# Router logits and expert rows from scaled rows, with the norm applied as a column per token

## The chip, the cores and the metric

The kernel runs on one core of one Trainium2 chip. The metric is the device time of one execution in microseconds. The kernel before was run three times: 1560.26 us is the median (1556.66 to 1560.38).

## What is computed

One inference step of a small diffusion backbone: two layers, 128 context tokens and 256 latent tokens, model width 1024. All is float32. Each layer has an attention branch and a recurrent branch, merged and projected with `w_out`, and then a mixture of experts. What matters here is the step into the experts:

```python
x = x + g1 * (merged @ lp['w_out'])
h2 = _rmsnorm(x, lp['norm2']) * (1 + sc2) + sh2
x = x + g2 * _moe(h2, router_w, router_b, lp['w_gate_up'], lp['w_down'])
```

`_rmsnorm` divides each token's row by its root mean square (rms) and multiplies by a gain per column. `sc2` and `sh2` are vectors per stream (context and latent) that come from a modulation product. In `_moe`, sigmoid scores of `h2 @ router_w` pick one group of four experts and in it two of 16 experts for each token. The expert is SwiGLU with 512 hidden columns. The modulation vectors of a layer come from twelve chunks of a product with `w_ada`; the gains and shifts of the first norm of a layer are chunks 0 to 3.

## The kernel before, in words

The kernel is written by hand, engine by engine. Each engine has a program in order, and semaphores (`wait_ge`, `then_inc`) link them. Line numbers are those of the profile.

- Activations are kept transposed: `xT` and `hT` are [128 partitions, 8 column tiles, 384 tokens]. Large products are done in three parts with a high and a low half of each operand. ScalarE rounds the weights to the high half (L1071, L1269), VectorE subtracts to get the low half (L1547, L1901).
- `w_ada`, `w_in` and the projections come as chunks of 2 MB into three slots of `ring`. Expert weights come as pieces of 1 MB into eight spots; six of these are halves of the ring slots, two lie in `parts`. SP issues all of these loads in the order of `chunk_order`, each when the last user of its spot is done (L481 to L484).
- Product results go through three banks `G`, taken in the order of `gemm_order`; transposes and small sums go through two banks `TB`, in the order of `tran_order`. The reader of a bank increments `gbank_read` or `tbank_read`, and TensorE waits for that before it uses the bank again.
- The output stage of a layer is three rows of eight split products (L545): `ap` (attention), `rp` (recurrent) and `wo` (output). `ADA_AFTER` puts modulation products (L555) and their sums (L564) between them.
- After each `wo` product VectorE adds it to `xT` (L1738) and squares the tile (L1742); TensorE sums the squares over partitions with a matrix of ones (L571), one product behind.
- After `wo` 7 the chain is: the last sum of squares, the root on ScalarE (`rms`, L1046), the load of the Exp table (L1231), the reciprocal of the [128, 384] tile `rs` (L1511), eight multiplications into `hT` (L1518), gain and shift on GpSimd for the context tokens (L2028) and on ScalarE for the latent ones (L1081), eight router products with 32 columns of weights (L777), a copy (L1237), the turn back to token rows (L791) and the sigmoid's exponential (L1249). Then VectorE routes: some fifty small steps from L1755 to L1855.
- Meanwhile TensorE does modulation products 2 and 3 of the next layer and their sums (layer 0), or five filler products (layer 1, `run_on`, L520: products whose result nobody reads).
- TensorE also transposes `hT` to token rows (24 transposes in six groups, L785); ScalarE copies each group (L1245) and stores the rows to `h2_rows` in DRAM (L1253, three stores).
- The rank of each token in its expert (L806) and the token of each place (L814) come from small products; L819 places the gates. Then GpSimd gathers the 128 rows of each expert with an indirect DMA (L2047). Unused places gather row 0. TensorE transposes them (L827), ScalarE copies (L1274), and the first expert product starts (L855, L861).
- The results of 14 experts are stored to `expert_rows`, those of the last two are kept on chip. At the end GpSimd gathers for each token the two rows (six indirect DMAs, L2060; picks of the kept experts read row 0 with gate 0), ScalarE and VectorE combine them (L1309, L1956), and TensorE transposes them (L959) and adds the kept experts (L964).

Of the kernel before, what the change touches and what calls it, by code (L numbers as in the profile page):

```python
# [33 lines left out]
CAP = 128  # L34
HELD = 2
# [90 lines left out]
def gemm_order():  # L126

    o = [(0, "ada", c) for c in ADA_START]
    for l in range(DEPTH):
# [28 lines left out]
def tran_order():  # L158
# [3 lines left out]
    for l in range(DEPTH):  # L162
# [6 lines left out]
        if l + 1 < DEPTH:  # L169
            o += [(l + 1, "mod", c) for c in ADA_FIRST]  # L170
# [10 lines left out]
def build(nc, x_prompt, x_sample, cache_k, cache_v, state_h, c, c_ctx, norm1_g, norm2_g, w_ada, b_ada,  # L181
# [4 lines left out]
    with ctx:  # L186
# [80 lines left out]
        shift_k = sb("shift_k", [P, KVH, 2])  # L267
        slot_gate = sb("slot_gate", [P, EVEN])
# [66 lines left out]
        same_b = tmp[:, 0, 0:6 * EVEN].rearrange("p (i b) -> p i b", i=6)  # L335
        hot_f = hot_c.bitcast(F32)
        gate_b = tmp[:, 1, 0:6 * EVEN].rearrange("p (i b) -> p i b", i=6)
# [8 lines left out]
        h2d = nc.dram_tensor("h2_rows", (T, D), F32, kind="Internal").ap()  # L346
        yd = nc.dram_tensor("expert_rows", (SENT * CAP, D), F32, kind="Internal").ap()

# [155 lines left out]
        def _(pe):  # L504
# [119 lines left out]
            for l in range(DEPTH):  # L624
# [6 lines left out]
                def h_ready(k):  # L631
                    pe.wait_ge(S("h_ready_p"), 2 * l * KT + k + 1)
                    pe.wait_ge(S("h_ready_a"), 2 * l * KT + k + 1)
# [114 lines left out]

                pe.wait_ge(S("att_split"), (l + 1) * HEADS)
                for name, high, low in (("ap", parts_r[:, 0], parts_r[:, 1]), ("rp", qT_r, gr_r),  # L750
                                        ("wo", parts_r[:, 0], parts_r[:, 1])):
                    for n in range(KT):
# [5 lines left out]
                        if n and name == "wo":  # L758
                            square_sum(gr, n - 1, slice(0, T), sq_base + n)
                        for plan, do in ((ADA_SUM_AFTER, mod_sum), (ADA_AFTER, modulation)):  # L760
# [11 lines left out]
                bank = g_take((l, "logits", 0))  # L772
                for k in range(KT):
                    pe.wait_ge(S("h_ready_p"), (2 * l + 1) * KT + k + 1)
# [1367 lines left out]
```

## Time and profile before

| | |
|---|---|
| median of 3 runs | 1560.26 us (1556.66 to 1560.38) |
| profiled execution | 1560.94 us |
| its span, first to last instruction | 1559.1 us |
| TensorE busy | 1496.3 us, 96% |
| VectorE busy | 1116.7 us, 72% |
| ScalarE busy | 921.6 us, 59% |
| GpSimd busy | 161.2 us, 10% |
| mean granted TensorE clock | 0.986 |
| moved by DMA | 373.00 MB, 239 GB/s on average |

The busy share is an average over stages. A stage's limit is read from the chain of waits: followed back from the last instruction, it gives at each moment the work that the end depended on. The granted clock is in parts of full speed (2.4 GHz).

### The profile page before, as it was taken

What the parts mean: (1) busy time and instruction counts of PE and PEld (TensorE: products, weight loads), DVE (VectorE), ACT (ScalarE), POOL (GpSimd) and SP (SyncE); (2) the same over time, 40 slices, a digit from 0 to 9 for tenths busy, and PEclk for the clock granted to TensorE, in tenths of its full rate; (3) what the DMA queues carried; (4) which work ended last, traced back from release to release, by engine and by line L of the source; (5) the groups of instructions that cost most, each with busy time, mean ns of one, the idle gap of its engine ahead of it and who ended that gap; (6) DMA issues with size and microseconds to landing.
All of it is one profiled execution on the core that took longest, in us unless ns stands there. A gap on an engine that the chain in (4) does not pass through costs nothing.

```text
span 1559.1 us, 19489 instructions
## 1 busy us (share of the span) xinstructions
PE 1496.3 (96%) x7375; PEld 1196.6 (77%) x7375; DVE 1116.7 (72%) x1717; ACT 921.6 (59%) x1176; POOL 161.2 (10%) x218
## 2 busy tenths in 40 slices
PE   6999999999998999999999999999999899999996
PEld 4699866679875788888769987666989478888885
DVE  4447656774646999999874665777464689999986
ACT  1233569972224877787742355999321577878774
POOL 0100012200011000000240000221000201000002
PEclk9999999999999999999999999999999999999999
DMA  9455433214667999999755553113240799999983
GB/s 348 172 201 199 147 108 112 68 56 162 216 224 293 360 401 410 409 407 406 290 189 194 191 186 140 63 63 113 97 174 12 288 355 408 413 412 406 406 346 122
DMA packets 132708, 373.00 MB, mean 239 GB/s; under 512 B 9217, under 2 KB 12673, under 8 KB 132609
## 3 DMA queue, kind: packets, MB, share of 16 engines
q1 hardware_dynamic: 113728, 326.57, 55.7%
q0 software_dynamic: 10432, 25.18, 4.6%
q10 hardware_dynamic: 8448, 19.94, 3.2%
q8 instruction: 62, 1.02, 0.3%
q14 instruction: 38, 0.30, 0.1%
HBM read 351.71 MB, written 19.94 MB: 238 GB/s over the span
## 4 chain that ended last, share of the span: by engine, by line
PE 78%; DVE 7%; ACT 5%; DMA 5%; issue 4%; POOL 1%; SPq 0%; POOLq 0%; DVEq 0%; ACTq 0%
PE bank L545 24%; PE bank L855 19%; PE bank L861 10%; PE bank L534 10%; PE bank L555 2%; DMA ring<-in_w_ada 2%; PE bank L743 2%; PE bank L827 2%; PE bank L716 1%; PE bank L571 1%; DMA expert_rows<-gb 1%; PE bank L653 1%; PE bank L648 1%; PE bank L564 1%; DMA tmp<-expert_rows,posu 1%
## 5 line engine op out<-in xcount | busy, mean ns | idle before, releaser
L1901 DVE TENSOR_TENSOR spot_low<-spot,piece_high 128x2048 fp32r<-128x2048 f32 x192 | 433.4, 2286 | 31.5 <-ACT piece_high L1269 30.5
L1269 ACT ACTIVATE piece_high<-spot 128x2048 fp32r<-128x2048 f32 x192 | 366.5, 1917 | 42.4 <-PE bank L861 40.3
L855 PE MATMUL bank<-piece_high,ga_r 128*128 128x512 f32 x768 | 308.8, 402 | 3.0 <-ACT ga_r L1286 1.4
L855 PE MATMUL bank<-spot_low,ga_r 128*128 128x512 f32 x768 | 301.6, 393 | 0.0
L861 PE MATMUL bank<-piece_high,ga_r 128*128 128x512 f32 x768 | 210.7, 396 | 0.0
L545 PE MATMUL bank<-parts_r,ga_r 128*128 128x384 f32 x768 | 202.6, 345 | 0.0
L534 PE MATMUL bank<-hT,ring 128*128 128x384 f32 x544 | 185.0, 494 | 4.4 <-ACT ga L1212 2.3
L855 PEld LDWEIGHTS bank<-piece_high,ga_r 128*128 128x128 f32 x768 | 144.3, 188 | 37.9 <-ACT ga_r L1274 2.2
L861 PEld LDWEIGHTS bank<-piece_high,ga_r 128*128 128x128 f32 x768 | 144.2, 188 | 34.5
L855 PEld LDWEIGHTS bank<-spot_low,ga_r 128*128 128x128 f32 x768 | 144.6, 188 | 30.6
L534 PEld LDWEIGHTS bank<-hT,ring 128*128 128x128 f32 x544 | 102.1, 193 | 71.2 <-issue 4.1
L545 PEld LDWEIGHTS bank<-parts_r,ga_r 128*128 128x128 f32 x768 | 138.3, 188 | 5.9 <-issue 5.0
L545 PE MATMUL bank<-parts_r,gb_r 128*128 128x384 f32 x384 | 129.7, 338 | 0.0
L545 PE MATMUL bank<-parts_r,hT_r 128*128 128x384 f32 x384 | 100.4, 342 | 0.0
L2047 POOL DMA_INDIRECT gr<-h_rows,ids x32 | 45.3, 1417 | 457.4 <-PE bank L827 423.7
L545 PE MATMUL bank<-parts_r,ring_r 128*128 128x384 f32 x256 | 87.9, 343 | 0.0
L1547 DVE TENSOR_TENSOR gb_r<-ring,ga_r 128x1024 fp32r<-128x1024 f32 x48 | 58.5, 1222 | 35.3 <-ACT ga_r L1071 33.7
L2040 POOL DMA_DIRECT2D gatew<-in_lru_wa x64 | 34.0, 536 | 465.3 <-PE bank L743 465.1
L545 PEld LDWEIGHTS bank<-parts_r,gb_r 128*128 128x128 f32 x384 | 72.1, 188 | 0.0
L545 PEld LDWEIGHTS bank<-parts_r,hT_r 128*128 128x128 f32 x384 | 69.4, 188 | 2.5
L1042 ACT ACTIVATE tmp<-bank 128x512 f32<-128x512 f32 x24 | 14.4, 598 | 83.7 <-PE bank L555 83.7
L1071 ACT ACTIVATE hT_r<-ring 128x1024 fp32r<-128x1024 f32 x36 | 37.1, 1052 | 36.6 <-PE bank L545 36.6
(314 smaller groups left out, 2351.7 us busy)
## 6 DMA issues: line engine op xcount, KB each, us to landing
spot<-in_w_gate_up SPq DMA_DIRECT2D x128, 1024.0 KB, 8.1
spot<-in_w_down SPq DMA_DIRECT2D x64, 1024.0 KB, 8.2
ring<-in_w_ada SPq DMA_DIRECT2D x24, 2048.0 KB, 8.1
ring<-in_w_in SPq DMA_DIRECT2D x22, 2048.0 KB, 8.1
expert_rows<-gb ACTq DMA_DIRECT2D x28, 512.0 KB, 6.9
ring<-in_w_attn_proj SPq DMA_DIRECT2D x4, 2048.0 KB, 8.3
ring<-in_w_rnn_proj SPq DMA_DIRECT2D x4, 2048.0 KB, 10.0
ring<-in_w_out SPq DMA_DIRECT2D x4, 2048.0 KB, 12.5
```

The costliest lines, as they stand in the source:

```text
L534: mm = pe.matmul(bank[:, 0:width], slot_kn(slot)[:, k, n * P:(n + 1) * P], rhs(k), start=(k == 0), stop=(k == KT - 1))
L545: mm = pe.matmul(bank[:, 0:T], w[:, k, :], x[:, k, :], start=(k == 0 and i == 0), stop=(k == KT - 1 and i == 2))
L555: mm = pe.matmul(bank[g:g + 32, :], cpad[:, k, :], slot_kn(s)[:, k, :], start=(k < 4), stop=(k >= 4), tile_position=(0, g))
L743: pe.matmul(bank[:, 0:CW], gatew[:, which, n % 2, :], xc[:, j, :], start=True, stop=True).then_inc(S("gemm_done"), 1)
L855: pe.matmul(out[n], high[:, 2 * q + k, :], w[:, k, n * 512:(n + 1) * 512], start=(q == 0 and k == 0 and i == 0), stop=False)
L861: mm = pe.matmul(out[n], low[:, 2 * q + k, :], w_high[:, k, n * 512:(n + 1) * 512], start=False, stop=(q == pieces - 1 and k == 1))
L1071: ac.activation(w_high_part(kind, n), slot_kn(s)[:, :, n % 4 * P:(n % 4 + 1) * P], ACT.Copy)\
L1269: ac.activation(highs[p % HIGHS], spots[u], ACT.Copy).then_inc(S("piece_high"), 1)
L1547: ve.tensor_tensor(low, slot_kn(s)[:, :, n % 4 * P:(n % 4 + 1) * P], high.bitcast(F32), ALU.subtract)\
L1901: ve.tensor_tensor(spots_low[u], spots[u], highs[p % HIGHS].bitcast(F32), ALU.subtract)\
L2040: po.dma_start(gatew[half * 64:half * 64 + 64, which, n % 2, half * 64:half * 64 + 64], w[l, d, 2 * j + half]).then_inc(S(f"gatew_loaded{n ...
L2047: po.indirect_dma_start(out=dst, out_offset=None, in_=h2d[:, :], in_offset=bass.IndirectOffsetOnAxis(ap=idx, axis=0)).then_inc(sem, 16)
```

## The change

- The norm is no longer applied to `h2` before the router. After each `wo` product, GpSimd (context) and ScalarE (latent) write the tile times gain into `xc` (`scaled`). The eight router products read `xc` and follow `wo` 7; the last sum of squares stands between the seventh and the eighth.
- The rms row is turned into a column per token with three one-row products; VectorE takes the reciprocal of [128, 3] (`rstd_c`). The exponential takes it as its scale, and `sel_e` has a minus sign. ScalarE's copies of the transposed rows take it as their scale.
- The shift enters as one-row products of the rms row with a row of shift values: for the logits `bias_row`, for the token rows `shift_row`. They are prepared in the `rp` stage: the router's product with the shift after `rp` 0 (`shift_logits`), its sum after `rp` 3 (`bias_turned`), and two transposes of the shift, copied by VectorE, stored to DRAM by ScalarE at `rp` 6 and loaded back as one row at `wo` 4.
- The six groups of transposes accumulate a product of one row and 512 columns each.
- Modulation products 2 and 3 of the next layer move from ahead of the router to behind the rank product (in place of four filler products in layer 0), their sums to behind the gate product, in place of one filler product. In layer 1 the five fillers ahead of the router go, and two of the last ones stay of three. The two fillers before the rank go in both layers. ScalarE's copies of the two products stand behind the first high piece of expert 0; VectorE's additions stand behind `slot_gate`.
- The gathers get a bounds check: unused places have an index past the last row (`NOWHERE`) and are not fetched; in the last gathers the picks of the kept experts are not fetched.

```diff
@@ gemm_order, tran_order
+        o.append((l, "logits", 0))
         if l + 1 < DEPTH:
             o += [(l + 1, "ada", c) for c in (2, 3)]
-        o.append((l, "logits", 0))
...
         o += [(l, "ids", 0)]
+        if l + 1 < DEPTH:
+            o += [(l + 1, "mod", c) for c in ADA_FIRST[2:4]]
@@ TensorE
+                def shift_logits():
+                    pe.wait_ge(S("exp_done"), (l + 1) * len(UNITS))
+                    t_read(pe, (l, "mod", 7))
+                    for k in range(KT):
+                        g = 32 * (k % 4)
+                        mm = pe.matmul(SB[0][g:g + 32, 0:2], rw[:, k, :], modT[:, 24 + k, :],
+                                       start=(k < 4), stop=(k >= 4), tile_position=(0, g))
+                    for st in range(2):
+                        mm = pe.transpose(SB[0][0:KT, (st + 1) * P:(st + 2) * P], modT[:, 24:32, st], ident)
+                    mm.then_inc(S("shift_logits"), 1)
+
+                def bias_turned():
+                    pe.wait_ge(S("bias_part"), l + 1)
+                    for st in range(2):
+                        mm = pe.matmul(SB[0][0:1, 16 + st * NE:16 + (st + 1) * NE], bias_part[:, st:st + 1], sel_e,
+                                       start=True, stop=True, skip_group_check=True)
+                    mm.then_inc(S("bias_turned"), 1)
...
+                for k in range(KT - 1):
+                    raw_logits(k)
                 square_sum(gr, KT - 1, slice(0, T), sq_base + KT).then_inc(S("ss_done"), 1)
-                if l + 1 < DEPTH:
-                    modulation(l + 1, 2)
-                    modulation(l + 1, 3)
-                    mod_sum(l + 1, 2)
-                    mod_sum(l + 1, 3)
-                else:
-                    run_on(SB[1], 5)
...
+                raw_logits(KT - 1).then_inc(S("gemm_done"), 1)
+
+                pe.wait_ge(S("rms_ready"), 2 * l + 2)
+                for t in range(TT):
+                    mm = pe.matmul(SB[1][:, t:t + 1], rs[0:1, t * P:(t + 1) * P], ones[0:1, 0:1],
+                                   start=True, stop=True, skip_group_check=True)
+                mm.then_inc(S("rms_turned"), 1)
+                g_read(pe, (l, "logits", 0))
+                pe.wait_ge(S("bias_known"), l + 1)
+                for t in range(TT):
+                    st = 0 if t == 0 else 1
+                    out = SB[0][:, t * NE:(t + 1) * NE]
+                    pe.matmul(out, lpart[:, t * P:(t + 1) * P], sel_e, start=True, stop=False, skip_group_check=True)
+                    mm = pe.matmul(out, rs[0:1, t * P:(t + 1) * P], bias_row[:, st * NE:(st + 1) * NE],
+                                   start=False, stop=True, skip_group_check=True)
+                mm.then_inc(S("logits_turned"), 1)
+
+                pe.wait_ge(S("shift_back"), 16 * (l + 1))
+                for i in range(2 * TT):
+                    t, half = divmod(i, 2)
                     bank = t_take((l, "h2", i))
                     for k in range(4):
+                        pe.matmul(bank[:, k * P:(k + 1) * P], xc[:, half * 4 + k, t * P:(t + 1) * P], ident,
+                                  is_transpose=True, start=(k == 0), stop=False, skip_group_check=True)
+                    pe.matmul(bank[:, :], rs[0:1, t * P:(t + 1) * P], shift_row[:, min(t, 1), half * 512:(half + 1) * 512],
+                              start=False, stop=True, skip_group_check=True).then_inc(S("tran_done"), 1)
...
-                run_on(SB[1], 2, T)
...
-                run_on(SB[1], 4)
+                if l + 1 < DEPTH:
+                    modulation(l + 1, 2)
+                    modulation(l + 1, 3)
+                else:
+                    run_on(SB[1], 4)
...
-                run_on(SB[1], 3)
+                if l + 1 < DEPTH:
+                    mod_sum(l + 1, 2)
+                    mod_sum(l + 1, 3)
+                run_on(SB[1], 2)
                 xturn(0)
@@ ScalarE
+                def scaled(k):
+                    g_read(ac, (l, "wo", k))
+                    ac.activation(xc[:, k, CTX:T], xT[:, k, CTX:T], ACT.Copy, scale=modA[:, 1, k, 1:2])\
+                        .then_inc(S("router_a"), 1)
...
+                ac.wait_ge(S("rstd_known"), l + 1)
+                ac.wait_ge(S("logits_turned"), l + 1)
+                for t in range(TT):
+                    ins = ac.activation(rt[:, 0, t, :], SB[0][:, t * NE:(t + 1) * NE], ACT.Exp, scale=rstd_c[:, t:t + 1])
+                ins.then_inc(S("logits_exp"), 1)
...
-                for q in range(3):
-                    piece_high("gu0", q)
+                piece_high("gu0", 0)
+                if l + 1 < DEPTH:
+                    ada_copy(l + 1, 2)
+                    ada_copy(l + 1, 3)
+                piece_high("gu0", 1)
+                piece_high("gu0", 2)
@@ VectorE
-                normed()
-                if l + 1 < DEPTH:
-                    mod_add(l + 1, 2)
-                    mod_add(l + 1, 3)
-                    ve.nop().then_inc(S("first_mods"), 2)
-
+                bank = g_ready(ve, (l, "logits", 0))
+                ve.tensor_copy(lpart, bank[:, 0:T]).then_inc(g_free((l, "logits", 0)), 1)
+                ve.wait_ge(S("rms_turned"), l + 1)
+                ve.reciprocal(rstd_c[:, :], SB[1][:, 0:TT]).then_inc(S("rstd_known"), 1)
@@ GpSimd
-                modulated(1)
+                for k in range(KT):
+                    g_read(po, (l, "wo", k))
+                    po.tensor_scalar(xc[:, k, 0:CTX], xT[:, k, 0:CTX], modA[:, 1, k, 0:1], None, ALU.mult)\
+                        .then_inc(S("router_p"), 1)
...
                     po.indirect_dma_start(out=dst, out_offset=None, in_=h2d[:, :],
-                                          in_offset=bass.IndirectOffsetOnAxis(ap=idx, axis=0)).then_inc(sem, 16)
+                                          in_offset=bass.IndirectOffsetOnAxis(ap=idx, axis=0),
+                                          bounds_check=T - 1, oob_is_err=False).then_inc(sem, 16)
```

## Rows read from the trace of the kernel before

**Rows 1.** Busy time by windows, in the experts: PE, PEld, DVE, ACT, POOL, PEclk, DMA, GB/s

```profile
600.00:700.00 100.00, 100.00 (x468) 81.67 (x467) 91.85 (x56) 78.82 (x56) 7.29 (x6) 1.00 1.02 408
```

**Rows 2.** Chain of waits, layer 0: start us, us, what

```profile
455.04 0.75 DVE xT L1738 x2
...
456.43 0.93 PE bank L571 x2
...
457.90 2.56 DVE hyb L1511
...
464.16 4.07 PE bank L777 x14
...
468.86 0.86 PE bank L791 x6
...
469.98 0.20 DVE pt L1755
...
477.24 0.25 DVE pt L1814
...
482.05 0.81 PE bank L814 x6
...
488.57 0.89 PE bank L827 x8
...
490.56 2.13 PE bank L855 x8
```

**Rows 3.** Chain of waits, layer 1

```profile
1205.43 0.75 DVE xT L1738 x2
...
1220.01 0.20 DVE pt L1755
...
1232.10 1.23 PE bank L814 x6
...
1240.25 0.89 PE bank L827 x8
...
1242.23 2.12 PE bank L855 x8
```

**Rows 4.** Timeline, layer 0, ScalarE and VectorE: start, us, engine, line, operation

```profile
457.89 1.28 ACT L1231 ACT_TABLE_LOAD   x1
...
484.34 4.48 DVE L1901 TENSOR_TENSOR spot_low<-spot,piece_high 128x2048 fp32r<-128x2048 f32 x2
```

**Rows 5.** Timeline, layer 0, TensorE

```profile
469.55 1.07 PE L785 MATMUL bank<-con,hT 128*128 128x128 f32 x8
...
476.44 3.68 PE L520 MATMUL bank<-con 128*128 128x512 f32 x8
```

**Rows 6.** Gathers (layer 0), last store (layer 1), its landing, gathers' landing

```profile
483.71 1.05 POOL L2047 DMA_INDIRECT gr<-h_rows,ids  x1 [16.66 <-DVE ids L1857]
...
485.06 2.41 POOL L2047 DMA_INDIRECT gr<-h_rows,ids  x1 [0.30 <-issue]
...
1224.04 0.33 ACTq L1253 DMA_DIRECT2D h_rows<-gr  x1
...
h_rows<-gr ACTq DMA_DIRECT2D x1, 512.0 KB, 8.2
...
DMA to landing us min/median/max: 4.1/7.7/10.3
```

**Rows 7.** Chain of waits, rnn projection stage, layer 1

```profile
1151.35 12.76 PE bank L545 x72
```

**Rows 8.** Timeline, layer 0, end of the experts: GpSimd and TensorE

```profile
777.72 0.94 POOL L2060 DMA_INDIRECT tmp<-expert_rows,posu  x1 [0.30 <-issue]
...
786.23 0.30 PE L959 MATMUL bank<-con,gb 128*128 128x128 f32 x1 [1.33 <-DVE tmp L1956]
```

**Rows 9.** Busy time by windows, columns as in rows 1

```profile
465.00:467.00 2.00, 2.00 (x10) 0.79 (x10) 0.66 (x5) 0.50 (x2) 2.00 (x5) 0.50 1.03 414
1232.00:1234.00 2.00, 1.90 (x10) 1.93 (x11) 0.43 (x3) 0.00 (x0) 0.17 (x1) 0.58 0.03 8
```

More of the change, by code:

```diff
@@ L34 @@
 CAP = 128
+NOWHERE = 512
 HELD = 2
@@ L169, in tran_order @@
         if l + 1 < DEPTH:
-            o += [(l + 1, "mod", c) for c in ADA_FIRST]
+            o += [(l + 1, "mod", c) for c in ADA_FIRST[0:2]]
         o += [(l, "h2", i) for i in range(2 * TT)]
@@ L779, in _, with raw_logits @@
-                mm.then_inc(S("gemm_done"), 1)
-                def h2_rows(i):
+                logits = g_take((l, "logits", 0))
+                def raw_logits(k):
+                    pe.wait_ge(S("router_p"), l * KT + k + 1)
+                    pe.wait_ge(S("router_a"), l * KT + k + 1)
+                    g = 32 * (k % 4)
+                    return pe.matmul(logits[g:g + 32, 0:T], rw[:, k, :], xc[:, k, 0:T],
+                                     start=(k < 4), stop=(k >= 4), tile_position=(0, g))
@@ L790, in _ @@
-                for t in range(TT):
-                    mm = pe.matmul(OB[:, t * NE:(t + 1) * NE], lpart[:, t * P:(t + 1) * P], sel_e,
-                                   start=True, stop=True, skip_group_check=True)
-                mm.then_inc(S("logits_turned"), 1)
-                for i in range(1, 2 * TT):
-                    h2_rows(i)
+                        pe.matmul(bank[:, k * P:(k + 1) * P], xc[:, half * 4 + k, t * P:(t + 1) * P], ident,
+                                  is_transpose=True, start=(k == 0), stop=False, skip_group_check=True)
@@ L869, in xturn @@
                         for b in range(2):
-                            pe.wait_ge(S(f"tbank_read{b}"), len(range(b, T_AT[(l, "ids", 0)] + 1, 2)))
+                            last = T_AT[(l + 1, "mod", 3) if l + 1 < DEPTH else (l, "ids", 0)]
+                            pe.wait_ge(S(f"tbank_read{b}"), len(range(b, last + 1, 2)))
                     else:
@@ L878, in gu @@
                     if e == 0:
-                        done = G_AT[(l, "logits", 0)]
+                        done = G_AT[(l + 1, "ada", 3) if l + 1 < DEPTH else (l, "logits", 0)]
                         for b in range(2):
@@ L1503, in mod_add @@
                     link(ve.tensor_copy(modA[:, 3, kk:kk + 4, :], m))
-            norms = [0]
-            def rstd():
-                norms[0] += 1
-                ve.wait_ge(S("rms_ready"), norms[0])
-                link(ve.reciprocal(rs, rs))
             for l in range(DEPTH):
-                def normed():
-                    rstd()
-                    for k in range(KT):
-                        ve.tensor_tensor(hT[:, k, :], xT[:, k, :], rs, ALU.mult).then_inc(S("xn_ready"), 1)
                 if l == 0:
@@ L2020, in _ @@
             for l in range(DEPTH):
-                def modulated(which):
-                    base = (2 * l + which) * KT
-                    for k in range(KT):
-                        if which == 0 and k % 4 == 0:
-                            po.wait_ge(S("first_mods"), 2 * l + k // 4 + 1)
-                        po.wait_ge(S("xn_ready"), base + k + 1)
-                        po.tensor_scalar(hT[:, k, 0:CTX], hT[:, k, 0:CTX], modA[:, which, k, 0:1],
-                                         modT[:, which * 24 + k, 0:1], ALU.mult, ALU.add).then_inc(S("h_ready_p"), 1)
-                modulated(0)
+                for k in range(KT):
+                    if k % 4 == 0:
+                        po.wait_ge(S("first_mods"), 2 * l + k // 4 + 1)
+                    po.wait_ge(S("xn_ready"), l * KT + k + 1)
+                    po.tensor_scalar(hT[:, k, 0:CTX], hT[:, k, 0:CTX], modA[:, 0, k, 0:1],
+                                     modT[:, k, 0:1], ALU.mult, ALU.add).then_inc(S("h_ready_p"), 1)
                 for n, (d, j) in enumerate(PAIRS):
```

105 lines of the change are left out of this document (57 added, 48 removed).

## The prediction

> **What bounds the kernel now.** I read the busy time by windows first: in the middle of the experts TensorE is busy for all of 100 us [rows 1]. The DMA engines are full there too, but a piece of weights is requested only when TensorE has given a spot back, so TensorE sets the pace, and fewer gathered bytes give nothing in that stretch. The change has to pay elsewhere: in the stretch between the last output product of a layer and its first expert product. There I read the chain of waits [rows 2, 3]. In both layers it is serial: one engine works, the next waits. From the update of x after product wo 7 (call its start T0: 455.04 and 1205.43) to the first expert product there are 490.56 - 455.04 = 35.5 us in layer 0 and 1242.23 - 1205.43 = 36.8 us in layer 1. The routing on VectorE starts at T0 + 14.94 and T0 + 14.58.
>
> **Removed: the norm ahead of the router.** Before, the chain from T0 is: update and square 1.39, last sum of squares and root 1.47, reciprocal of the 128x384 tile 2.56, normalising, modulating and the eight router products until 468.16, a copy, the turn back 0.86, the exponential, VectorE at 469.98 [rows 2]. The new chain, from the same rows:
> - Seven of the eight raw router products run while VectorE updates and squares tile 7. They are 14 instructions. Six products of the turn back took 0.86 with their drain, some 0.12 apart. So they need 1.6 us and have a gap of 1.39; the sum of squares starts at T0 + 1.55. The bounds of the delay are 0 and 0.6: GpSimd may scale tile 7 first and hold up the squaring, and its steps paced seven router products in 4.07, 0.58 each [rows 2].
> - Sum and root, 1.47: T0 + 3.0.
> - rms turned into columns: three one-row products, six instructions like the turn back, 0.8 to the last. The logits need six full and six one-row instructions more, another 1.5 us: T0 + 5.3. VectorE's copy of the logits and the small reciprocal lie beside this, and so does the load of the Exp table, 1.28 us from T0 + 3.0 [rows 4].
> - Three exponentials in place of one, 0.25 each (the one before lay between 469.72 and 469.98): routing starts at T0 + 6.05.
>
> That is 8.9 us (layer 0) and 8.5 us (layer 1) earlier.
>
> **Added: shift rows in the transposes.** TensorE now has six groups, each of four transposes (eight transposes took 1.07, so 0.45) and a one-row product 512 wide. No row shows a product with one row of weights. I take that of the full 128x512, whose eight instructions took 3.68 [rows 5], so 0.86 for two; the lower bound is the 0.12 spacing, the upper double time at half clock. One group is 1.3 and six are 7.8: TensorE ends at T0 + 13.1, ScalarE copies the last by T0 + 13.85 (a copy twice as wide, with its hand-over, took 1242.23 - 1240.25 - 0.89 = 1.1 [rows 3]), and nine narrow rank products, 0.45 as an estimate, give VectorE its input at T0 + 14.3. VectorE alone would be there at 6.05 + (477.24 - 469.98) = 13.3. So one microsecond is given back: **the transposes are late next**. The rank is read at T0 + 14.3 against 22.2 and 21.85, a gain of 7.9 and, with the same steps in layer 1, 7.5. The work up to the ids product is unchanged (482.05 - 477.24 = 4.8): ids product at T0 + 19.1.
>
> **Moved: modulation products 2 and 3 of the next layer.** They left a place where TensorE waited for the reciprocal, so nothing is gained there. In layer 0 they take the place of four filler products of the same length between rank and ids; in layer 1 nothing changes. The two sums (16 small instructions, 1.9) replace one filler (0.9). VectorE's two additions, eight steps of about 0.2, now stand ahead of its first low halves (4.48 for two, [rows 4]); these finish by T0 + 29, before the rows of expert 0 are split. On ScalarE the copies stand between two pieces that wait for nothing urgent. On SP the pieces of expert 1 now wait for product 3, until T0 + 18.3 instead of about T0 + 6; they are needed only after expert 0's eleven microseconds of products, so this costs nothing directly.
>
> **Rows for expert 0.** The gather waits for the ids and for the h2 stores. Before, in layer 1, the last store was issued at 1224.04 and landed 8.2 later, at 1232.2, one microsecond ahead of the gather at 1233.8 [rows 6]. That slack is gone: the chain has become shorter than the stores allow.
> - Layer 1: last store at T0 + 13.95, landed 22.15, gather 22.7. Eight 1 MB pieces are issued from T0 on; with the stores that is 10 MB, at the 408 GB/s of rows 1 until about T0 + 25.7. With DMA idle a gather took 4.9 us from its issue at 483.71 to the transposes at 488.57 [rows 2, 6]; over all gathers, most in full traffic, the median landing is 7.7. Fewer rows are fetched (48 of 128 on average), so I take 5.1: transposes at T0 + 27.8 against 1240.25 - 1205.43 = 34.8. Gain 7.0.
> - Layer 0: only four pieces lie in the way of the stores, so ids bound it: gather at T0 + 20.8 (483.71 - 482.05 behind the ids product). But expert 1's pieces, requested from T0 + 17 on, collide with it. I take 6.5 between 4.9 and 7.7: rows at 27.3. TensorE itself has ids, gates, sums and two fillers to do, 5.8 us from T0 + 19.1 at full clock and twice that at half: free between 24.9 and 30.7. I take 28.3 for the transposes, against 488.57 - 455.04 = 33.5. Gain 5.2.
>
> Here the trace shows a lock. The first gather's issue took 1.05 us; the second, beside VectorE's low halves (both inputs in SBUF), took 2.41 [rows 4, 6]. The Trainium skill (SBUF — State Buffer, "SBUF: two separate sides") says that such VectorE work keeps GpSimd from writing its descriptors; the trace agrees. By that rule the later gather of layer 1 would meet the low halves and lose 1.4 us, and the total gain below would be 8.6 instead of 10.0.
>
> **Added earlier: products of the shift.** After product rp 0 come eight router products of two columns (16 instructions) and two transposes, after rp 3 two products for the sums. That stage has no gap on TensorE: 72 products in 12.76 us without one [rows 7]. The nearest row is the turn back, 0.12 for each with full weights; the weights here have 32 columns. I take 1.6 per layer, bounds 0.8 and 2.6. VectorE's three copies, ScalarE's two small transfers and GpSimd's eight scalings lie in idle time: products last 4.2 us each. **Cost 3.2.**
>
> **Combine.** At the layer's end TensorE waited 1.33 for the last combined rows; their six gathers are issued one behind the other, 0.94 each when clear [rows 8]. Rows that belong to the two held experts are now skipped. Bounds: 1.3 gained per layer, or a slower checked gather. I take 0.5, 1.0 in all.
>
> **Sum.** 7.0 + 5.2 - 3.2 + 1.0 = 10.0 us. The profiled execution took 1560.94 (span 1559.1 and 1.8 around it), 0.7 above the median of 1560.26. 1560.94 - 10.0 = **1551.0**.
>
> **Rivals.**
> - **The clock of TensorE falls in the new chain.** In layer 0 the granted clock was 0.50 at 465 to 467, after the narrow products; in layer 1 it was 0.58 at 1232, after a short idle [rows 9], and the ids products took 1.23 instead of 0.81 [rows 2, 3]. 0.50 is 1.2 GHz. Between T0 + 2.2 and T0 + 5.3 there are only narrow products. If four of the six groups ran at half speed, the rank would come 5.2 later. The ids product would start at T0 + 24.3. Layer 1 would then lose nothing to its stores and have its transposes at 31.2 (gain 3.6), layer 0 at 31.5 (gain 2.0): 5.6 - 3.2 + 1.0 = 3.4, 1557.5. Against it: in layer 1, sparse transposes from 1219 on did not bring the clock down, and the groups are dense. The Trainium skill (TensorE: Matmul & The Clock Gate, "What's actually happening") says that throttled is the default and activity lifts it, which speaks for this rival. Chance 0.12.
> - **DMA keeps the rows back.** Stores and gathers in full traffic take their longest. With 7.7 for both gathers and 2 us more for layer 1's last store the transposes come at 32.4 in layer 1 (gain 2.4) and, TensorE being late too, 29.5 in layer 0 (gain 4.0): 6.4 - 3.2 + 1.0 = 4.2, 1556.7. For it: the slack of one microsecond [rows 6]. Against it: fewer rows. Chance 0.10.
> - **Slower: gathers with a bounds check.** No row shows one. If GpSimd needs longer for each, the six serial gathers at the end of a layer carry it in full, since TensorE already waits there [rows 8], and the first gather carries it once. With 1.5 us more each: 7 x 1.5 x 2 = 21, less the 1.0 that I counted: 10.0 - 1.0 - 21 = -12, 1573. It decides from 9.0 / 14 = 0.64 us more per gather. Against it: the check compares 128 numbers. Chance 0.08.
> - **Better than forecast.** The shift products cost 0.8 per layer (1.6 more), the combine gains its 1.3 twice (1.6 more), and one-row products that cost less than full ones take the transposes out of the rank's way (1.5 more): 14.7 in all, 1546.2. Chance 0.12.
>
> The forecast itself has 0.58. A measurement of this kernel can tell about 0.3% (4.7 us) from no change, so faster means under 1555.6. It holds the forecast but for 0.03, the better case, and a quarter of the first two rivals: 0.55 + 0.12 + 0.06 = 0.73. Slower is the third rival and 0.02 of accidents: 0.10. The rest, 0.17, is the same. The range leaves out the slower rival and a little below: 1545 to 1559.
>
> **What would show it.** Routing on VectorE starting near T0 + 6, and the rank read near T0 + 14.3, right after the sixth copied group; the sixth group ending near T0 + 13. In layer 1 a gather that waits for a store, not for ids. First expert product at T0 + 30 in both layers. 1.6 us of small products in the rp stage. Six gathers at the end, each near 0.94 to 2.5. I am wrong if the groups take over 2 us each (clock), if the first expert product comes after T0 + 33, or if the checked gathers take over 0.6 us more.

## The result and the profile after

The forecast was wrong in sign. The changed kernel took 1570.9 us (median of 4, 1568.64 to 1572.53) against 1558.5 for the kernel before on the same chip (4 runs, 1556.66 to 1560.38). The ratio is 1.0076 [1.0058 to 1.0094], slower by about 12 us, and the forecast had been 1551.0 with a range to 1559. Its profiled execution took 1572.27 us, 11.3 more than the 1560.94 of the one before.

The page of the changed kernel, lines on busy time, granted clock by 40 slices and bytes:

```profile
span 1570.4 us, 19661 instructions
...
PE 1517.8 (97%) x7437; PEld 1205.0 (77%) x7437; DVE 1106.5 (70%) x1707; ACT 922.6 (59%) x1178; POOL 166.2 (11%) x218
...
PEclk9999999999996999999999999999999699999999
...
DMA packets 132763, 361.96 MB, mean 230 GB/s; under 512 B 11951, under 2 KB 15439, under 8 KB 132659
```

TensorE is busy 21.5 us longer than the 1496.3 of before; 11 MB fewer are moved; and the clock line has a 6 in two of its slices. These are the ones in which the rows of expert 0 are prepared, one in each layer. The chain of waits of the changed kernel (start us, us, what), layer 0 and then layer 1; L827 are the transposes of a group, L829 its two one-row shift products:

```profile
461.67 0.59 PE bank L827 x4
462.25 1.05 PE bank L829 x2
...
465.74 1.05 PE bank L827 x4
466.78 2.00 PE bank L829 x2
...
478.70 0.41 PE bank L840 x9
479.12 6.25 PE bank L563 x32
485.37 0.78 PE bank L852 x6
...
487.22 8.28 DMA gr<-h_rows,ids
...
495.54 1.97 PE bank L865 x8
...
499.21 2.98 PE bank L893 x8
...
1221.58 0.84 PE bank L827 x4
1222.41 2.00 PE bank L829 x2
...
1240.43 0.41 PE bank L840 x9
1240.84 6.00 PE bank L528 x8
1246.84 0.58 PE bank L852 x6
...
1248.42 4.25 DMA gr<-h_rows,ids
...
1254.92 2.13 PE bank L893 x8
```

The chain follows TensorE through all six groups. The first group takes 0.59 + 1.05 = 1.64 us, from the third on each takes 1.05 + 2.00 = 3.05, and the modulation products behind the rank take 6.25. Before, the same 32 instructions took 3.64, ahead of the router:

```profile
457.27 3.64 PE L555 MATMUL bank<-ring,cpad 128*32 128x512 f32 x32
```

In layer 1, eight full filler instructions (L528) take 6.00 in the same place; they took 3.68 before.

The busy time by windows shows the clock (columns as in [rows 9]; the number ahead of the last two is the granted clock):

```profile
460.00:465.00 5.00, 5.00 (x23) 2.93 (x22) 2.26 (x13) 1.53 (x6) 0.00 (x0) 0.90 1.03 416
465.00:470.00 5.00, 5.00 (x12) 2.17 (x12) 4.03 (x21) 1.38 (x2) 0.00 (x0) 0.50 0.73 292
...
1230.00:1235.00 5.00, 5.00 (x12) 2.40 (x12) 0.00 (x0) 1.38 (x2) 0.00 (x0) 0.50 1.00 384
```

In the last two TensorE is busy for the whole window, and its clock is 0.50, that is 1.2 GHz. It fell while TensorE was working without a gap: from 455 to 475 every window of 5 us shows it busy for 5.00. The low clock also outlasts the groups, so that the full-row products behind them are slow at first.

Against T0, the start of VectorE's update of x after wo 7 (455.34 and 1215.25 now):

| | layer 0 before | layer 0 after | layer 1 before | layer 1 after |
|---|---|---|---|---|
| routing starts | +14.9 | +7.1 | +14.6 | +7.1 |
| rank products | +21.2 | +23.4 | +20.8 | +25.2 |
| ids product | +27.0 | +30.0 | +26.7 | +31.6 |
| expert 0's transposes | +33.5 | +40.2 | +34.8 | +37.5 |
| first expert product | +35.5 | +43.9 | +36.8 | +39.7 |

The differences between the two chains add up to the whole. The first expert product of layer 0 comes at 499.21 instead of 490.56 (+8.65). From there to T0 of layer 1 it is 716.04 instead of 714.87 (+1.17). Then 39.67 instead of 36.80 (+2.87), and the tail to the end of the span is 315.48 instead of 316.87 (-1.39): 11.3 us in sum.

### The profile page after: what moved, and what is told of

Same layout as the page of the kernel before. It is cut to its first block, busy times and chain, and to the rows that moved or that the text cites. A ratio compares the mean times of both kernels' runs of the same rounds, so it can differ in the third digit from the quotient of the medians.

```text
span 1570.4 us, 19661 instructions
## 1 busy us (share of the span) xinstructions
PE 1517.8 (97%) x7437; PEld 1205.0 (77%) x7437; DVE 1106.5 (70%) x1707; ACT 922.6 (59%) x1178; POOL 166.2 (11%) x218
## 3 DMA queue, kind: packets, MB, share of 16 engines
q8 instruction: 64, 1.05, 0.3%
## 4 chain that ended last, share of the span: by engine, by line
PE 79%; issue 8%; DVE 4%; DMA 4%; ACT 4%; POOL 1%; POOLq 0%; SPq 0%; DVEq 0%; ACTq 0%
PE bank L553 24%; PE bank L893 18%; PE bank L542 10%; PE bank L899 9%; PE bank L563 3%; DMA ring<-in_w_ada 2%; PE bank L751 2%; PE bank L865 2%; PE bank L829 1%; PE bank L724 1%; PE bank L579 1%; PE bank L661 1%; PE bank L656 1%; PE bank L572 1%; DMA gr<-h_rows,ids 1%
## 5 line engine op out<-in xcount | busy, mean ns | idle before, releaser
L2096 POOL DMA_INDIRECT gr<-h_rows,ids x32 | 38.7, 1210 | 496.9 <-PE bank L865 434.9
L563 PE MATMUL bank<-ring,cpad 128*32 128x512 f32 x384 | 50.3, 647 | 4.5 <-DMA ring<-in_w_ada 4.3
```

What stands on the lines that cost most here:

```text
L563: mm = pe.matmul(bank[g:g + 32, :], cpad[:, k, :], slot_kn(s)[:, k, :], start=(k < 4), stop=(k >= 4), tile_position=(0, g))
L2096: po.indirect_dma_start(out=dst, out_offset=None, in_=h2d[:, :], in_offset=bass.IndirectOffsetOnAxis(ap=idx, axis=0), bounds_check=T - 1, ...
```

## The experiments

Each ratio below is taken against the kernel before on the same chip. The versions ran on different chips, so the ratios compare them better than the medians do.

**Theory A**: products that use few rows of the array don't keep TensorE's clock up, however densely they are issued; 128 rows would. **Rival B**: the short products and the waits ahead of the groups bring the clock down, and anything dense and full ahead of them would prevent it. **Rival C**: the order of transfers is what costs, since the pieces of expert 1 now meet the gather. **Rival D**: the bounds check.

### Shift products on 128 rows, and left out

```diff
-        shift_row = gbf[0:1, 1024:3072].rearrange("a (s n) -> a s n", s=2)
+        shift_row = gbf[:, 1024:3072].rearrange("a (s n) -> a s n", s=2)
...
-                    pe.matmul(bank[:, :], rs[0:1, t * P:(t + 1) * P], shift_row[:, min(t, 1), half * 512:(half + 1) * 512],
+                    pe.matmul(bank[:, :], rs[:, t * P:(t + 1) * P], shift_row[:, min(t, 1), half * 512:(half + 1) * 512],
```

All rows of `rs` are alike, so with the shift divided by 128 the sum is the same. The shift row is loaded to all 128 partitions for this. The second version has no shift product in the groups at all, so the shift is missing from its token rows.

> Theory A (one-row products do not count as work for TensorE's clock, so the clock falls to 1.2 GHz in the six transpose groups and stays there): with the same product on 128 rows (the shift divided by 128 in every row, the rms row is already in all 128) the groups run at 2.4 GHz, one takes 1.3 to 1.6 us in place of 3.05, the rank is read at T0 + 15 to 16 in both layers, and the kernel takes 1550 to 1556. Theory B (the clock falls because the narrow products and the gaps between T0 + 2 and T0 + 6 have taken the place of dense filler products; the rows of the groups do not matter): the groups still take about 3 us and the time stays within 2 us of 1571. Theory C (the moved loads that collide with the gather are the main loss): layer 0 stays behind by 3 us or more even with fast groups.

> The shift is left out of the token rows; the rest is the changed kernel. Theory A: no one-row product 512 wide is left, the groups are 0.6 us of transposes paced by ScalarE's copy of 0.7, the clock does not fall in them, the rank is read at T0 + 13.5 and the time is 1548 to 1554. Theory B: the clock falls all the same, at T0 + 7 or 8, and with groups of 1.1 us at half clock the time is 1554 to 1560; transposes alone would then show a granted clock of 0.5 in their stretch.

Full rows: 1553.9 us, ratio 0.9970 [0.9952 to 0.9988]; without the products: 1551.3, 0.9960 [0.9946 to 0.9974]. Six products a layer on 128 rows in place of one are worth 17 us (the ratios differ by 0.0106). The chain of the version with full rows, a group in the middle and the rank:

```profile
465.12 0.44 PE bank L827 x4
465.55 0.86 PE bank L829 x2
...
471.08 0.40 PE bank L840 x9
```

A group takes 1.30 us, what I had priced, and in layer 0 the rank product comes at T0 + 15.0. In layer 1 it comes at T0 + 18.3. There the clock fell with the first group all the same, but it rose again in the midst of them. The windows of layer 1:

```profile
1210.00:1215.00 5.00, 5.00 (x13) 2.72 (x13) 3.82 (x20) 1.25 (x4) 0.00 (x0) 0.50 1.03 416
1215.00:1220.00 5.00, 5.00 (x24) 3.25 (x23) 2.46 (x14) 2.66 (x4) 0.00 (x0) 0.94 0.99 368
```

So the clock rose while TensorE did nothing but groups with full rows: the first took 1.05 + 1.71, the fourth 0.44 + 0.86. In the version without shift products TensorE had little to do beside the routing (2.90 of 5 us at 465 to 470), and the clock fell to 0.50 at 470 to 475. That cost less: the routing set the rank, at T0 + 13.3, and only the modulation products behind it were slow (6.18).

### The same substitution in the kernel before

```diff
-                    pe.matmul(bank[:, 0:width], ident, con[:, 256:256 + width], start=True, stop=True)
+                    pe.matmul(bank[:, 0:width], ident[0:1, :], con[0:1, 256:256 + width], start=True, stop=True)
```

This is the kernel before, with nothing of the change in it; only its filler products have one row of weights and one of data.

> The kernel before with its dense filler products cut from 128 rows to one row; nothing reads them, and their number and width stay. Theory A (one-row products do not count for TensorE's clock): in layer 1, where the kernel before held 2.4 GHz from T0 to T0 + 26 with five, two and four fillers, the granted clock now falls to 0.5 between T0 + 4 and T0 + 10 and stays there, as it did in layer 0 behind the narrow products; the first expert product of layer 1 comes 1 to 4 us later and the kernel takes 1557 to 1563 where the kernel before takes 1557. Rival (what counts is that TensorE is issued instructions, whatever their rows): the clock in the same stretch stays as before and so does the time, within 1 us.

1575.3 us, ratio 1.0107 [1.0074 to 1.0140]: A holds without the change, and by more than I had expected (1557 to 1563). A window of it in layer 0, and then its chain:

```profile
480.00:485.00 5.00, 5.00 (x15) 2.84 (x13) 1.47 (x8) 0.00 (x0) 0.22 (x1) 0.50 0.11 43
```

```profile
475.39 0.39 PE bank L806 x9
475.77 7.12 PE bank L520 x8
482.89 1.39 PE bank L814 x6
...
496.17 3.71 PE bank L855 x8
```

The fillers between rank and ids, 3.68 us in [rows 5], now take 7.12 and hold up the ids product; the first expert product comes at T0 + 42.0 instead of 35.5, and in layer 1 at T0 + 42.2 instead of 36.8. The fillers compute nothing that anyone reads. With full rows the granted clock was 1.00 and 0.98 from 475 to 485, with one row 0.50.

### Dense work ahead of the groups; modulation products back in front

```diff
+                pe.wait_ge(S("rstd_known"), l + 1)
+                run_on(SB[1], 4)
                 pe.wait_ge(S("shift_back"), 16 * (l + 1))
```

> Four dense filler products of 128 rows stand between the turned logits and the six groups, nothing else is changed. Theory B: the clock stays at 2.4 GHz through the groups (1.6 us each in place of 3.05), the rank comes 8 - 3.5 = 4 to 5 us earlier in each layer, and the time falls to 1560 to 1563. Theory A: the clock falls during the one-row products, a few us later than before; the fillers cost 3.4 us and give two or three groups at full clock back, so the time is 1569 to 1574.

> Modulation products 2 and 3 go back ahead of the router's turn (their sums stay behind), four fillers return behind the rank. Only layer 0 changes. Theory C: expert 1's pieces are requested 17 us earlier, the gather of expert 0 lands 4.5 us after its issue in place of 8.3, and the time falls by 1 us or more although the routing starts 3 us later. Theory A: the routing starts 3 us later but the groups are the bound and they shift by 3.6 too, the rank comes 3 to 4 later, the gather is faster by 3 to 4, and the time stays within 2 us of 1571; the clock falls in the groups as before.

Four full filler products ahead of the groups: 1569.1 us, 1.0088 [1.0057 to 1.0119], no better than the changed kernel. Its chain in layer 0 shows how long they help (L829 are the transposes and L831 the shift products here):

```profile
460.85 3.63 PE bank L528 x8
...
468.19 1.05 PE bank L831 x2
469.24 0.59 PE bank L829 x4
469.83 1.97 PE bank L831 x2
```

Three groups run at full clock instead of one, then the clock falls. B is out as the cause: dense work ahead only puts the fall off. With the modulation products of layer 1 back behind the router products, ahead of the turned rms row, and fillers behind the rank the time is 1568.6, 1.0072 [1.0051 to 1.0093]. All six groups of layer 0 then ran at half clock, the routing started at T0 + 10.5 instead of 7.1 and the rank came at 28.4. But the gathered rows landed 4.1 us after the issue, against 8.3. That is C's collision. It is real, but it was not the larger term.

### How many rows

The same product on 32 and on 64 rows, with the shift divided by as much.

> The changed kernel with the shift product of the six groups on 32 rows of weights, every value divided by 32 (the changed kernel has one row, the full version 128). Theory A says that what TensorE's clock goes by is more than time spent streaming columns: a product that uses few rows counts for little. If it counts in proportion to its rows, 32 of 128 is near one row: the groups fall to the granted clock of 0.50, a group takes about 3.05 us, the rank product comes after T0 + 22 and the time is within 3 us of the changed kernel's, 1568 to 1573. If any row group that is filled counts as full, it behaves as the version with 128 rows: rank at T0 + 15, 1553 to 1556. In between, with the clock falling late in the groups: 1558 to 1565. I take the first as the likelier, at 0.6, the last at 0.25.

> The changed kernel with the shift product of the six groups on 64 rows of weights, values divided by 64. One row and 32 rows both gave groups at the granted clock of 0.50, 128 rows gave 1.00 for most of them. If a product counts in proportion to its rows, half the rows should lie between: the clock falls later or in only some groups, rank product between T0 + 16 and T0 + 21, 1557 to 1565. If anything short of all rows counts as little, it is like 32 rows: rank at T0 + 23 to 26, 1567 to 1571. If half is enough, 1552 to 1556. I hold the first likeliest, 0.5, the other two 0.3 and 0.2.

32 rows: 1568.9 us, 1.0061 [1.0045 to 1.0077], not to be told from one row. 64 rows: 1565.9, 1.0055 [1.0025 to 1.0085], but its ten runs lie between 1556.27 and 1575.83, far wider than any other version's. Its profiled run has both outcomes in one execution. The windows with the groups of layer 0 and of layer 1:

```profile
465.00:470.00 5.00, 5.00 (x12) 2.42 (x12) 4.28 (x24) 1.38 (x2) 0.00 (x0) 0.50 0.71 281
...
1220.00:1225.00 5.00, 5.00 (x25) 3.17 (x24) 2.19 (x12) 1.85 (x6) 0.00 (x0) 1.00 1.03 417
1225.00:1230.00 5.00, 5.00 (x19) 2.14 (x18) 4.26 (x23) 2.06 (x3) 0.00 (x0) 1.00 1.03 375
```

The same instructions run once at 0.50 (rank at T0 + 24.9) and once at 1.00 (rank at T0 + 16.9). I had held a late fall within the groups for likeliest. What came is either the one or the other for a whole layer.

In layer 1 of that run, at full clock, the chain of waits shows another thing:

```profile
1222.57 1.05 PE bank L829 x2
1223.62 0.58 PE bank L827 x4
```

At the same clock the group costs 1.63 with 64 rows, as the first of one row did, and 1.30 with 128. The instructions themselves are alike: the shortest took 592 ns with 128 rows, 589 with 64 and 587 with 32 and with one. The Trainium skill (TensorE: Matmul & The Clock Gate, "Why this matters for your kernels") says that a single product of 32 rows takes the time of one of 128. The records agree with it at a given clock. But a group with few-row products costs 0.33 more, and the clock comes on top. The 0.33 seems to be the price of changing between few rows and 128: three one-row products of one column with nothing between them (L809) took 0.75 us, and on 128 rows 0.76.

### The collision and the bounds check

```diff
                 if (l, name) in PIECE_AT:
+                    if name == "gu1.0":
+                        sy.wait_ge(S("row_gathered0"), 16 * (l * NE // 2 + 1))
```

SP holds the pieces of expert 1 until the first gathered rows have landed. This was added to the version with full rows, to the kernel before, and to the changed kernel alone.

> The full-row version in which SP holds back the pieces of expert 1 until the first gathered rows have landed. Theory C, second part (the gather and the stores lose to weight traffic once the chain is shorter): the first gather lands 4 to 4.5 us after its issue in both layers in place of 7.9 and 5.6, the last store of layer 1 lands before the ids, the first expert product comes at T0 + 28.5 to 29.5 in layer 0 and T0 + 30 to 31 in layer 1 in place of 32.4 and 34.1, and the kernel takes 1546 to 1549. Rival: the pieces held back are then late for expert 1 or 2 and TensorE waits for them; what is gained ahead of expert 0 is lost there, and the time stays within 1.5 us of 1554.

> The kernel before with the same hold, as a control. Its gathers were issued 28.5 us after T0, when the pieces had landed, and its last store landed 0.2 to 1.1 us ahead of the ids. Theory: the hold gives it nothing (the time is within 1.5 us of the 1557 of the kernel before) or costs up to 3 us if expert 1 waits for its pieces. Rival: the kernel before was also held by its stores, and the hold gains 1 us or more in it too.

> The changed kernel, one-row products kept, with one wait added on SP: the pieces of expert 1 are requested only when the first gathered rows of expert 0 have landed. Theory C (the moved modulation products push these requests onto the gather) says: in layer 0 the gather lands 4.0 to 4.6 us after its issue instead of 8.4, the transposes of expert 0 start near T0 + 36.5 instead of T0 + 40.2 (the sums at half clock may hold them back to T0 + 38), and the time falls by 2 to 4 us, to 1567 to 1569. Layer 1, where the pieces were long under way, gains under 1 us. If the collision is only a coincidence of the profile, the time does not move. Either way the clock stays at 0.50 in the groups, as in the changed kernel.

With full rows: 1551.6 us, 0.9936 [0.9913 to 0.9959] against 0.9970 without the hold. The intervals overlap by a little, and I had expected 1546 to 1549. In the kernel before it gives nothing: 1559.1, 0.9997 [0.9978 to 1.0016]. In the changed kernel alone 1568.1, 1.0061 [1.0044 to 1.0077]: some 2 us by the ratio, less than that interval is wide. There the rows of layer 0 landed 4.4 us after the issue, but TensorE was late to take them. Its chain:

```profile
481.92 5.25 PE bank L565 x32
...
489.29 1.77 PE bank L574 x16
491.06 2.45 PE bank L530 x4
493.51 1.96 PE bank L867 x8
```

The DMA step of 8.28 us is gone from the chain. The sums of the modulation (L574) and two fillers (L530) stand in its place: a wait for data was exchanged for one for TensorE's own work. The first expert product of layer 0 comes at T0 + 40.8 instead of 43.9.

The version with full rows and without bounds checks (unused places gather row 0 again):

> The full-row version without the bounds checks: unused places gather row 0 again, picks of the kept experts too. If the skipped rows help: the time rises from 1554 by 1 to 4 us, the first gather of layer 0 lands 0.5 to 1.5 us later than the 7.9 of the full-row version, and the last rows to combine land later by 0.5 us. If the check costs GpSimd time (1.00 us in place of 0.94 for each issue in the profile): the time falls by less than 1 us. My theory: the rows help little, since expert stages are bound by TensorE; within 1.5 us of 1554.

1553.3 us, 0.9958 [0.9941 to 0.9974], against 1553.9 with them. D is out, and skipping rows gives nothing that can be measured either. In the profiles the check costs 0.6 us ahead of the first gather of layer 0: 1.05 from the start of the ids to it, 0.46 without.

### A better version

> The version with full shift rows and the hold on expert 1's pieces, and the rank products moved ahead of the last of the six groups. My prediction had said that the transposes are late next, by one microsecond. If that holds at full clock, the rank is read at VectorE's own pace, at T0 + 14.4 in place of T0 + 15.0 to 16.7, the last group and its store come later in its place, and at most 1 to 2 us are gained over both layers: 1549 to 1551, ratio to the kernel before about 0.993. If the last store is what the gather waits for, nothing is gained and layer 1 may lose 0.5. If TensorE idles while it waits for the picks and its clock falls for that, the last group and the ids product run at half speed and it is slower than the version without, 1553 or more.

> The changed kernel with only the short one-row products on 128 rows (rms turned to columns, the logits' bias); the six long shift products keep one row. If the long ones in the groups are what lets the clock fall, it is 1.00 for one or two groups longer and 0.50 after them: rank at T0 + 19 to 23, time 2 to 6 us under the changed kernel's 1570, so 1564 to 1568. If the short ones start the fall and the groups only keep it down, the clock stays at 1.00 in this version, the rank comes at T0 + 14, and the time is near the 1554 of the version with full shift rows. I hold the first for likelier, since the kernel before falls to 0.50 in a stretch of dense one-row fillers alone.

> The version with full shift rows, the hold and the rank product ahead of the last group, with the short products on 128 rows too, but with the two filler products ahead of expert 0 kept in layer 0. The version with both edits took 4 us less than the one with neither. If the clock made that difference, this one keeps it at 1.00 through the groups in both layers, has the rank at T0 + 12.8 and takes 1544 to 1546. If the two fillers made it, the rank stays at T0 + 14.5 to 16 in layer 0 and the time at 1547 to 1549. One more thing may show: with the fillers kept, the sums ahead of them may no longer find the clock at 0.50 at the start of expert 0.

> As the version before it in this list, and besides: the small one-row products ahead of the groups (rms turned to columns, logits' bias) on 128 rows with values divided by 128, and in layer 0 the two filler products between the sums of modulation and expert 0's transposes left out. If one-row products are what lets the clock fall ahead of the groups, full rows there keep it at 1.00 longer, and with the two fillers gone layer 0 starts expert 0 some 0.9 to 1.8 us earlier: 1547 to 1550. If these few small products weigh nothing in the clock (they are short with gaps between them), the gain is the two fillers' alone, under 1 us in layer 0 where the gather's landing sets the start, and the time is that of the version before it, within 1 us.

- Full rows, the hold, and the rank products ahead of the last group: 1548.1 us, 0.9918 [0.9902 to 0.9935].
- The same and the short one-row products on 128 rows as well: 1542.5 us (1541.89 to 1545.14), 0.9907 [0.9890 to 0.9924].
- The same and two fillers ahead of expert 0 left out in layer 0: 1544.2, 0.9899 [0.9881 to 0.9917]. The ratios don't tell these three apart; the medians of the last two are 4 to 6 us under the first's. With the fillers kept the time is no longer than without, so what shows in these medians is put down to the short products, and not to the fillers.
- The changed kernel with only the short products on 128 rows: 1569.2, 1.0070 [1.0046 to 1.0094], where I had said 1564 to 1568. All groups of layer 0 but the first run at half clock, and that one falls in its midst: the long products in the groups alone bring the clock down.

The short products seem to matter once the groups are full. With one-row short products the clock still fell at the end of them in some layers (0.67 at 460 to 465 in the first of these versions, where it rose again during the third group). With all on 128 rows it stayed up in the profiles: in the second version the windows show 1.00 from T0 to beyond the rank in both layers. The one with the rank in it, layer 0:

```profile
470.00:475.00 5.00, 4.35 (x41) 1.86 (x44) 4.41 (x23) 2.47 (x4) 0.00 (x0) 1.00 0.76 311
```

Its chain of waits now leads through VectorE's routing instead of the groups (L566 are the modulation products, L896 the first expert product):

```profile
463.58 0.61 ACT pt L1293 x3
...
464.22 0.20 DVE pt L1806
...
472.51 0.28 PE bank L845
472.79 3.57 PE bank L566 x32
...
485.74 2.14 PE bank L896 x8
```

The first expert product comes at T0 + 28.1 in layer 0 and T0 + 26.8 in layer 1, against 35.5 and 36.8 before. That is 7.4 and 10.0 us less. By its ratio the version takes 14.5 us less than the kernel before.

## Why the prediction was wrong, step by step

- **The step that failed**: "No row shows a product with one row of weights. I take that of the full 128x512." The duration at a given clock is nearly the same (587 ns against 592); what it does to the clock is not. The six groups were priced at 7.8 us at full clock. They took 16.3 in layer 0 and 18.1 in layer 1, mostly at the granted clock of 0.50. The same groups on 128 rows take 1.30 each at full clock, and the kernel with them takes 17 us less.
- **The rival that came true was too small in both its numbers.** "The clock of TensorE falls in the new chain" had a chance of 0.12 and half clock for four of six groups. The clock was down from the second group on (in layer 1 from the first) and for the modulation products too (6.25 us, 3.64 before), so its 1557.5 was 13 us too low. My argument against it was that "the groups are dense". They are, and it doesn't help. The rule I quoted, that activity lifts the clock, fits the runs; my reading of what is activity does not. I had also put nothing on the fillers that go. They are full-row products, and the kernel before loses 1.1% when they are not.
- **"Costs nothing directly"**, the move of expert 1's pieces onto the gather, was wrong as well. The forecast did count the collision with the gather, with 6.5 us for the landing, but it took 8.3. Holding the pieces gives the changed kernel some 2 us by the ratio, with an interval that also allows none, since TensorE itself was late.
- **Right**: the routing started at T0 + 7.1 (6.05 said). Of the difference, 0.6 is the eighth router product, which stands behind the last sum of squares (0.76 us; I had the turned rms row start without it), and the rest is the logits' products: 0.33 for each where one row and 128 alternate, and 0.22 with 128 throughout (routing at T0 + 6.5 then). Removing the norm is worth 7.5 to 7.9 us there, against 8.5 to 8.9 said. "The transposes are late next" held at full clock (rank product at T0 + 15.0 with full rows in layer 0; I had said that its result is read at 14.3), and moving the rank ahead of the last group took them out of the way.
- **Shift products**: 1.6 us per layer were said, as an estimate from full-weight products. The chain shows 0.24 + 0.32 us behind `rp` 0 and 0.16 behind `rp` 3, so 0.7. In layer 0 even that costs nothing, since TensorE then waits for the load of `w_out`, in both kernels. In layer 1 it is 0.7 of the +1.17 above. The term of 3.2 should have been 0.7. The timeline of the changed kernel in layer 1, and the wait in the chain of the kernel before in layer 0:

```profile
1139.91 0.31 PE L762 MATMUL bank<-modT,rw 128*32 128x2 f32 x16
1140.15 0.38 PE L765 MATMUL bank<-con,modT 128*8 128x128 f32 x2
...
393.38 12.54 DMA ring<-in_w_out
```

- **Combine**: 1.0 said for both layers; the tail behind layer 1's first expert product is 1.39 shorter. The wait for the last combined rows is 1.33 there instead of 1.84, and in layer 0 it is 1.33 as before, so the skipped rows have at most the 0.5 of it.
- **Slower by bounds-checked gathers**: the issue takes 1.00 instead of 0.94, where 0.64 more for each of seven gathers would have decided. Only the first gather of a layer comes 0.6 later. This rival foretold a slower kernel, but its mechanism did not occur.
- The late gather beside VectorE's low halves did occur where TensorE was fast: in layer 1 of the version with full rows the gather waited for its store, as foretold, and its issue took 2.88 us beside them (from 1229.44; the low halves run from 1229.04). The issue of the first gather takes 1.12 where they don't run. That is the lock of the Trainium skill (SBUF — State Buffer, "SBUF: two separate sides"); the trace agrees.
- **Slips in the working**: the slack of the last store in layer 1 was 1.6 us (1232.2 to 1233.8), not one. And the gains were taken off the profiled execution, 0.7 above the median. Neither changes the outcome.

Not settled: how the activity that holds the clock is counted. The runs have 1, 32, 64 and 128 rows of weights with 512 columns, always between full transposes; they don't separate rows in use from another property that changes with them, such as the number of moving elements. Nor does any run show why the clock fell in one layer or version and not in another with the same short products.

## What to carry to other kernels

A product with few rows took the time of a full one here, and a stretch of such products let TensorE fall to 1.2 GHz. What stood behind it took up to 1.7 times as long too (6.25 us instead of 3.64). To add a row vector to 128 rows, spread it over all 128 rows of weights (values divided by 128) instead of using one. When TensorE is fully busy and its part of the chain grows, read the granted clock of that window before looking for waits, and before removing fillers ask what their replacement does to it.

## What the runs showed of the hardware that I had not expected

- The clock fell to 0.50 under groups with products of one row or of 32, with TensorE busy for all of each window (changed kernel; the kernel before with one-row fillers too). It rose or held under the groups with 128 rows, and with 64 rows it did one or the other from layer to layer in one execution, with a spread of 19.6 us over ten runs.
- Where few-row and 128-row products alternate, a group of four transposes and one product (two instructions) takes 0.33 us more at full clock (1.63 against 1.30), and a small product of 16 columns 0.1 more (0.33 against 0.22).
- The first gather of layer 0 landed 8.3 us after its issue with the weight pieces of expert 1 under way, and 4.4 us after it when they were held back (the changed kernel without and with the hold).
